# Turning the rows of the last gate product by DMA in two planes of 16-bit words

## The reference, cut to what matters

```
x = x + (silu(h @ w_ffn_gate) * (h @ w_ffn_up)) @ w_ffn_down
gate = sigmoid(rmsnorm(x, ple_norm_g) @ w_ple_gate)      # (1024 x 1024) @ (1024 x 1024)
x = x + gate * (p @ w_ple_proj)                          # (1024 x 256) @ (256 x 1024)
out = rmsnorm(x, final_norm_g)
```

## Time and profile before

| | us |
|---|---|
| median of 3 runs (1244.51 to 1245.03) | 1244.6 |
| the profiled execution | 1244.54 |
| its span in the trace | 1242.8 |
| PE busy | 1228.3 (99%) |
| DVE busy | 714.8 (58%) |
| POOL busy | 511.4 (41%) |
| ACT busy | 472.5 (38%) |

### The profile page before, as it was taken

The page is one execution under the profiler, slowest core; times in us unless marked ns, Lnnn a source line. Parts: engine busy times, 40 slices in busy tenths (PEclk is TensorE's granted clock), DMA queues, the critical chain, the costliest instruction groups (busy, mean ns, idle before and its releaser), DMA issues.

```text
span 1242.8 us, 16468 instructions
## 1 busy us (share of the span) xinstructions
PE 1228.3 (99%) x5998; PEld 1037.0 (83%) x5998; DVE 714.8 (58%) x1160; ACT 472.5 (38%) x866; POOL 511.4 (41%) x508
## 2 busy tenths in 40 slices
PE   9999999999999999999999999999999999999997
PEld 8888888788998888888888888888888888888886
DVE  5644444366664347745544455444499999954434
ACT  6622222245554125533333333333354344424422
POOL 2533443351000004455543455433499889810001
PEclk9999999999999999999999999999999999999999
DMA  9511101001031400333342342422554455420002
GB/s 334 176 34 42 45 1 43 1 1 34 18 105 50 152 1 1 85 119 115 98 127 77 94 127 85 128 94 80 182 199 161 167 169 188 151 85 1 1 34 102
DMA packets 102063, 115.14 MB, mean 93 GB/s; under 512 B 4832, under 2 KB 67936, under 8 KB 101984
## 3 DMA queue, kind: packets, MB, share of 16 engines
q1 hardware_dynamic: 101552, 113.57, 28.2%
q10 hardware_dynamic: 432, 0.54, 0.1%
HBM read 90.49 MB, written 23.59 MB: 92 GB/s over the span
## 4 chain that ended last, share of the span: by engine, by line
PE 93%; DMA 2%; ACT 2%; DVE 1%; issue 1%; SPq 1%; POOL 0%; POOLq 0%; ACTq 0%; DVEq 0%
PE PS L1729 11%; PE PS L1728 11%; PE PS L1727 11%; PE PS L206 7%; PE PS L208 7%; PE PS L207 7%; PE PS L2061 5%; PE PS L2062 5%; PE PS L2063 5%; PE PS L1046 3%; PE PS L1069 3%; PE PS L2438 2%; PE PS L2440 2%; PE PS L2439 2%; PE PS L2453 2%; PE PS L880 1%
## 5 line engine op out<-in xcount | busy, mean ns | idle before, releaser
L206 PE MATMUL PS<-WF,HTH 128*128 128x512 f32 (+1 forms) x448 | 176.6, 394 | 1.2 <-DVE WF L184 0.9
L208 PE MATMUL PS<-WF,HTL 128*128 128x512 f32 (+1 forms) x448 | 173.3, 387 | 0.0
L207 PE MATMUL PS<-WF,HTH 128*128 128x512 f32 (+1 forms) x448 | 172.9, 386 | 0.0
L1448 DVE TENSOR_TENSOR X<-X,PS 128x512 f32<-128x512 f32 x172 | 110.2, 679 | 54.4 <-PE PS L208 37.2
L1727 PE MATMUL PS<-HTH,WF 128*128 128x512 f32 x336 | 130.7, 389 | 0.0
L1728 PE MATMUL PS<-HTL,WF 128*128 128x512 f32 x336 | 130.7, 389 | 0.0
L1729 PE MATMUL PS<-HTH,WF 128*128 128x512 f32 x336 | 130.7, 389 | 0.0
L1660 DVE TENSOR_TENSOR WF<-RAW,WF 128x512 fp32r<-128x512 f32 x63 | 69.8, 1109 | 77.2 <-ACT WF L1650 77.2
L206 PEld LDWEIGHTS PS<-WF,HTH 128*128 128x128 f32 x448 | 84.2, 188 | 17.5 <-issue 1.2
L1727 PE MATMUL PS<-WF 128*128 128x512 f32 x252 | 98.0, 389 | 0.0
L1728 PE MATMUL PS<-WF 128*128 128x512 f32 x252 | 98.0, 389 | 0.0
(11 more groups left out here) (268 smaller groups left out, 2778.4 us busy)
## 6 DMA issues: line engine op xcount, KB each, us to landing
hid<-TMP SPq DMA_DIRECT2D x74, 256.0 KB, 2.3
TMP<-hid SPq DMA_DIRECT2D x25, 512.0 KB, 4.5
RAW<-in_w_ffn_gate SPq DMA_DIRECT2D x22, 512.0 KB, 4.1
RAW<-in_w_ffn_up SPq DMA_DIRECT2D x22, 512.0 KB, 5.3
RAW<-in_w_ffn_down SPq DMA_DIRECT2D x22, 512.0 KB, 4.3
X<-in_x SPq DMA_DIRECT2D x16, 512.0 KB, 6.0
RAW<-in_w_in SPq DMA_DIRECT2D x32, 256.0 KB, 3.9
TAB<-hid SPq DMA_DIRECT2D x9, 512.0 KB, 4.7
```

The costliest lines, as they stand in the source:

```text
L206: nc.tensor.matmul(dst, HTH[:, k, tok], w_h, start=(k == 0), stop=False)
L207: nc.tensor.matmul(dst, HTH[:, k, tok], w_l, start=False, stop=False)
L208: last = nc.tensor.matmul(dst, HTL[:, k, tok], w_h, start=False, stop=(k == K - 1))
L1448: nc.vector.tensor_tensor(x, x, src, ALU.add).then_inc(done, 1)
```

## The change

The transposes on TensorE are left out. In their place, for each token tile, in this order:

1. POOL copies the 1024 words of 32 bits of a row of x into two planes of 1024 words of 16 bits (`x_split`), in TMP.
2. SP issues one DMA transpose of the 128 x 2048 words of 16 bits (`sp_x_turn`), into 16 blocks of 128 x 128, also in TMP.
3. POOL copies the two planes back together into words of 32 bits (`x_join`), in GB.
4. ACT and DVE make high and low part from there, at the same places of their queues as before (`joined_hi`, `joined_lo`).

There is one buffer for each of the three steps. The squares of ACT write their unused result to PSUM instead of TMP, and the load of the final gain into GB moves behind the last low part. Two semaphores of the attention (`a_mask`, `a_rec`) are merged into others with doubled counts; the order there is the same.

```
+        x_halves, x_turned, x_joined = sem("x_halves"), sem("x_turned"), sem("x_joined")
...
         def sp_6(e):
...
-            e.wait_ge(e_lo, 6)
+            for t in range(T):
+                sp_x_turn(e, t)
+            e.wait_ge(n_ple.lo, 2 * T)
             e.dma_start(GB[:, :], t_in["final_norm_g"].partition_broadcast(P)).then_inc(s_gain, 16)
...
+        def words_of(x):
+            return x.bitcast(U16).rearrange("p (n b) -> p b n", b=2)
+        HALVES, HALVES_T, JOINED = tmp(2048, 1024).bitcast(U16), tmp(3072, 1024).bitcast(U16), GB[:, :]
+        def x_split(e, t):
             if t == 0:
                 e.wait_ge(r_alo, STEPS)
+            else:
+                e.wait_ge(x_turned, 16 * t)
+            e.wait_ge(f_added, N_DOWN + 2 * t + 2)
+            nc.gpsimd.tensor_copy(HALVES.rearrange("p (b n) -> p b n", b=2), words_of(X3[:, t, :])).then_inc(x_halves, 1)
...
+        def sp_x_turn(e, t):
+            e.wait_ge(x_halves, t + 1)
             if t:
+                e.wait_ge(x_joined, t)
+            e.dma_start_transpose(HALVES_T.rearrange("p (c n) -> p c n", n=P), HALVES).then_inc(x_turned, 16)
...
+        def x_join(e, t):
+            e.wait_ge(x_turned, 16 * t + 16)
+            if t:
+                e.wait_ge(n_ple.lo, 2 * t)
+            else:
+                e.wait_ge(e_lo, 6)
+            nc.gpsimd.tensor_copy(words_of(JOINED), HALVES_T.rearrange("p (b n) -> p b n", b=2)).then_inc(x_joined, 1)
...
+        def joined_hi(e, t):
+            e.wait_ge(x_joined, t + 1)
+            for j in range(2):
+                nc.scalar.copy(HTH[:, 4 * j:4 * j + 4, t * P:t * P + P], joined(j)).then_inc(n_ple.hi, 1)
+        def joined_lo(e, t):
...
         def pool_6(e):
+            x_split(e, 0)
             for t in range(T):
                 norm_rstd(e, n_ple, t, 48)
+                x_join(e, t)
+                if t < T - 1:
+                    x_split(e, t + 1)
...
-            def turn(t):
-                if t in (4, 6):
-                    ple_turn(e, t // 2 - 2)
-            pe_down(e, turn)
-            ple_turn(e, 2)
+            pe_down(e)
...
-                if u < 5:
-                    ple_turn(e, u + 3)
```

More of the change, by code:

```diff
@@ L16 @@
 I32 = mybir.dt.int32
+U16 = mybir.dt.uint16
 ALU = mybir.AluOpType
@@ L131, in __init__ @@
                     self.lo = sem(name + "_lo")
-        n_mix, n_ple = Norm("mix", rows=False, turned=False), Norm("ple", rows=False)
+        n_mix, n_ple = Norm("mix", rows=False, turned=False), Norm("ple", rows=False, turned=False)
         n_ffn, n_out = Norm("ffn", split=False), Norm("final", turned=False, split=False)
@@ L849, in build @@
         a_proj, a_hi, a_lo = sem("a_proj"), sem("a_hi"), sem("a_lo")
-        a_scores, a_mask, a_max, a_bias = sem("a_scores"), sem("a_mask"), sem("a_max"), sem("a_bias")
-        a_exp, a_rec, a_prob, a_turn = sem("a_exp"), sem("a_rec"), sem("a_prob"), sem("a_turn")
+        a_scores, a_max, a_bias = sem("a_scores"), sem("a_max"), sem("a_bias")
+        a_exp, a_prob, a_turn = sem("a_exp"), sem("a_prob"), sem("a_turn")
         a_pt, a_pv, a_o_hi, a_o_lo = sem("a_pt"), sem("a_pv"), sem("a_o_hi"), sem("a_o_lo")
@@ L1050, in pe_turn @@
             t = n % T
-            e.wait_ge(a_prob, n + 1)
+            e.wait_ge(a_prob, 2 * n + 2)
             e.wait_ge(a_pt, n)
@@ L1160, in dve_biggest @@
             nb, width = seen(t)
-            nc.vector.memset(src[0:CHUNK, nb - 1, width - CHUNK:width], MASKED).then_inc(a_mask, 1)
-            e.wait_ge(a_mask, n + 1)
+            nc.vector.memset(src[0:CHUNK, nb - 1, width - CHUNK:width], MASKED).then_inc(a_max, 1)
+            e.wait_ge(a_max, 2 * n + 1)
             nc.vector.tensor_reduce(ST[:, 74 + t % 2:75 + t % 2], src, mybir.AxisListType.XY if nb > 1 else AXX,
                                     ALU.max).then_inc(a_max, 1)
-            e.wait_ge(a_max, n + 1)
+            e.wait_ge(a_max, 2 * n + 2)
             nc.vector.tensor_scalar(ST[:, 76 + t % 2:77 + t % 2], ST[:, 74 + t % 2:75 + t % 2], -SCALE, None,
@@ L1179, in dve_divide @@
             e.wait_ge(a_exp, n + 1)
-            nc.vector.reciprocal(ST[:, 80 + t % 2:81 + t % 2], ST[:, 78 + t % 2:79 + t % 2]).then_inc(a_rec, 1)
-            e.wait_ge(a_rec, n + 1)
+            nc.vector.reciprocal(ST[:, 80 + t % 2:81 + t % 2], ST[:, 78 + t % 2:79 + t % 2]).then_inc(a_prob, 1)
+            e.wait_ge(a_prob, 2 * n + 1)
             p = tmp((t % 2) * 1024, (t + 1) * P)
@@ L2091, in down_lo, with pe_down @@
                                     ALU.subtract).then_inc(d_lo, 1)
-        def pe_down(e, more):
+        def pe_down(e):
             e.wait_ge(d_lo, STEPS + 4)
@@ L2109, in pe_down @@
                     last.then_inc(f_down, 1)
-                more(t)
         def pe_5(e):
@@ L2247, in sp_6, with joined @@
                 e.wait_ge(s_out[c], 16 * T // 4 + (16 if c == 3 else 0))
+        SINK = PS[:, 0:2, :].rearrange("p b n -> p (b n)")
         def ple_squares(e, t):
             e.wait_ge(f_added, N_DOWN + 2 * t + 2)
+            if t:
+                e.wait_ge(n_ple.squares, t)
+            norm_squares(e, n_ple, t, 48, X3[:, t, :], SINK)
+        def words_of(x):
+            return x.bitcast(U16).rearrange("p (n b) -> p b n", b=2)
+        HALVES, HALVES_T, JOINED = tmp(2048, 1024).bitcast(U16), tmp(3072, 1024).bitcast(U16), GB[:, :]
+        def x_split(e, t):
             if t == 0:
                 e.wait_ge(r_alo, STEPS)
-            if t:
[L2254 to L2259, removed]
+            else:
[4 more added lines that the diff above has]
+            e.wait_ge(x_halves, t + 1)
+            if t:
+                e.wait_ge(x_joined, t)
+            e.dma_start_transpose(HALVES_T.rearrange("p (c n) -> p c n", n=P), HALVES).then_inc(x_turned, 16)
+        def x_join(e, t):
+            e.wait_ge(x_turned, 16 * t + 16)
+            if t:
+                e.wait_ge(n_ple.lo, 2 * t)
+            else:
+                e.wait_ge(e_lo, 6)
+            nc.gpsimd.tensor_copy(words_of(JOINED), HALVES_T.rearrange("p (b n) -> p b n", b=2)).then_inc(x_joined, 1)
+        def joined(j):
+            return JOINED[:, j * HALF:(j + 1) * HALF].rearrange("p (k n) -> p k n", k=4)
+        def joined_hi(e, t):
[3 more added lines that the diff above has]
+        def joined_lo(e, t):
+            d = slice(t * P, t * P + P)
+            for j in range(2):
+                e.wait_ge(n_ple.hi, 2 * t + j + 1)
+                nc.vector.tensor_tensor(HTL[:, 4 * j:4 * j + 4, d], joined(j), HTH[:, 4 * j:4 * j + 4, d].bitcast(F32),
+                                        ALU.subtract).then_inc(n_ple.lo, 1)
         def p_part(t, y):
@@ L2285, in act_6 @@
                 if t in (5, 7):
-                    turned_hi(e, n_ple, (t - 5) // 2)
-            turned_hi(e, n_ple, 2)
+                    joined_hi(e, (t - 5) // 2)
+            joined_hi(e, 2)
             for t in range(T):
@@ L2290, in act_6 @@
                 if 1 <= t <= 5:
-                    turned_hi(e, n_ple, t + 2)
+                    joined_hi(e, t + 2)
                 if t >= 1:
@@ L2313, in act_6 @@
                 n = HALF // 2
-                nc.scalar.activation(tmp(2048, n), X3[:, T - 1, HALF + i * n:HALF + i * n + n], ACT.Square, scale=D ** -0.5,
+                nc.scalar.activation(SINK[:, 0:n], X3[:, T - 1, HALF + i * n:HALF + i * n + n], ACT.Square, scale=D ** -0.5,
                                      accum_out=LAST_SUM if i else ST[:, 112 + T - 1:112 + T]).then_inc(n_out.squares, 1)
@@ L2328, in squares_half @@
                 e.wait_ge(n_out.squares, half * T + t)
-            nc.scalar.activation(tmp(2048, HALF), X3[:, t, half * HALF:(half + 1) * HALF], ACT.Square, scale=D ** -0.5,
+            nc.scalar.activation(SINK[:, 0:HALF], X3[:, t, half * HALF:(half + 1) * HALF], ACT.Square, scale=D ** -0.5,
                                  accum_out=ST[:, 96 + 16 * half + t:97 + 16 * half + t]).then_inc(n_out.squares, 1)
@@ L2360, in dve_6 @@
                 if t in (5, 7):
-                    turned_lo(e, n_ple, (t - 5) // 2)
-            turned_lo(e, n_ple, 2)
+                    joined_lo(e, (t - 5) // 2)
+            joined_lo(e, 2)
             for t in range(T):
@@ L2365, in dve_6 @@
                 if 1 <= t <= 5:
-                    turned_lo(e, n_ple, t + 2)
+                    joined_lo(e, t + 2)
                 if t >= 1:
```

## The result

| | before | after |
|---|---|---|
| median, us | 1244.55 (1244.39 to 1245.03) | 1252.9 (1251.87 to 1253.29) |
| ratio to before | | 1.0065, 95% interval 1.005 to 1.008 |
| span of the profiled execution, us | 1242.8 | 1251.0 |

The change makes the kernel slower by 0.65%, some 8.3 us. The direction, the place and the mechanism were forecast; the forecast size was +30.8 us, more than three times too much.

What follows compares the result with a forecast made beforehand. TensorE was taken to bound the kernel. Saving 7.0 us of transposes against 37.8 us of waiting for the ring gave net +30.8 us, 1244.54 to 1275.3 us; range 1249 to 1360, slower 0.86.

Steps and rivals of the forecast that it cites:

- What bounds the kernel, and what is saved: TensorE, busy 99% of the span, bounds; removing 64 transposes, 8 tiles at 0.87 us, saves 7.0 us on the path.
- the ring: Per tile, POOL splits, SP's DMA transpose lands, POOL joins, without overlap between tiles; forecast period 11.8 us.
- S: POOL's split copy of a tile into planes, counted by elements: 2.5 us.
- D: DMA transpose of a tile, issue to landing: 7.0 us; chance 0.24 for above 12 us, 0.62 for 3 to 12.
- J: POOL's copy joining the two turned planes, counted by elements at the pace of its known copy: 2.1 us.
- Where the ring meets TensorE: Gate step 6 waits until eight rings have joined tile 7: starts at 1199.2 instead of 1168.4, 30.8 us late.
- the prediction's second formula: Short ring: tile 1's join waits for tile 0's low part; gate step 6 starts at 1123.4 + 6P.
- P: Period of the ring: S + D + J plus 0.2 us of handovers, 11.8 us, against 6.8 us per gate step.
- the branch of the long ring: Eight rings counted from the first split at 1102.1 decide: tile 7 joined at 1102.1 + 8 x 11.8 = 1196.5.
- The queue order: On ACT and DVE, tile t+2's parts stand ahead of step t-1's sigmoid and multiplication; costs one further ring, steps 2 to 6.
- the fast rival: The ring is short and hidden: up to the full 7.0 us gained, 1237.6; chance 0.09 for a gain above 2.5 us.
- The clock: TensorE's clock may fall in 5 us gaps per step, which absorb it; 0 to 5 us at the end, range only.

## Why the prediction was right in kind and wrong in size

- **What bounds the kernel, and what is saved: right.** With the ring out of the way 6.7 us are gained, where 8 x 0.87 = 7.0 were counted.
- **The ring and its serial order: right.** S, D and J follow each other in the chain, and overlapping them gives the gain.
- **The price of the transpose: the step that failed.** D was taken as 7.0 us and measured 4.2. The sum priced a packet at 55 ns, the mean over queue 1, whose packets average 1.1 KB, and took 128 for each DMA engine. The count was right (130), the price was not. The last transpose alone has 54.8% of 16 x 5.1 us for its 2080 packets, 21.5 ns each, and 130 x 21.5 ns = 2.8 us for an engine. They overlap a little: from the first start to the last pass 2.6 us, which leaves 1.6 of the 4.2 us outside the packets. A packet of a quarter of the bytes cost two fifths. Both estimates that the prediction drew from the Trainium skill (Advanced Engine Details and Errata, section X-Bar Transpose (TRN2), and VectorE: DVE Perf Modes, section The three transpose paths) are off here, to either side: 1.4 us for the transfer was 2.6, some 200 GB/s, and sixteen blocks are 4.2 us and not 20.9. The second took the page's time for one block sixteen times; here blocks after the first eight cost 0.15 us each.
- **The copies: right in sum.** By elements and not by bytes; 1.89 and 2.50 us where 2.5 and 2.1 were taken. The higher price sat on the wrong one: the split is not slowed in this ring, where it meets the low part of the tile before in part only (it is in the run with two buffers, 2.34 us), and the join writes with a step.
- **Where the ring meets TensorE: right for this size.** With D = 4.2 and the rest of its numbers the prediction's second formula gives P = 9.0, 1123.4 + 54 = 1177.4, +9.0 us; with the measured copies it is 1118.6 + 2.5 + 6 x 8.6 + 2.7 = 1175.4, +7.0; measured was 1176.33, one ring being 0.7 us longer. So with the price of the transpose put right, and nothing else, the forecast is +9.0 where +8.3 was measured. The size fell in a gap of the reasoning all the same: the forecast worked in the branch of the long ring, 8P from the first split, where 3.2 us too much in P count eight times, and its ends of +2 and +71 us showed how much hung on one unknown.
- **The queue order: right in kind.** It was named as one further ring, which would be 8.6 us; undoing it in full gave 6.2 of the 8.3 us back. What it can give is about the 6.8 us of a gate step and not a ring, since step 7 then waits for the tile that step 6 waited for. That the low part of p stands in the same order was not seen, nor that for a short ring the limit binds at step 2. By this the fast rival was priced too well: at P = 6.35 us it gave 3 us and not 7.
- **The clock: the reasoning held, the place was not foreseen.** The prediction had it fall in gaps of 5 us a step and be taken up by them. Gaps of 1.5 us a step left the granted clock full (1.00 from 1150 to 1170). It fell once, in a standstill of 7.45 us that was not forecast, and TensorE waited for the ring behind it all the same. In the run with two transposes, gaps of 2.9 to 3.8 us had it at 0.70 to 0.78, and they did take it up.

## What to carry to other kernels

When work is taken from the engine that is the bound and spread over a chain of other engines with one buffer each, the period of the chain is the sum of its links and not the longest; second buffers were worth more here (from +8.3 to -6.1 us, one for the join of tile 1 among them) than the cheaper copies (to -3) or half the transpose (to +2). Look then at what the consumers have queued behind the late result: the same order that costs at most 0.6 us with a short ring makes 6.2 of the 8.3 us lost with a ring of 8.6 us. And a long wait in a profile may only be the first place where a loss shows; if removing it makes an equal one appear later, the cause lies behind both.

## What was not expected of the hardware

A DMA transpose of 128 x 2048 words of 16 bits within SBUF lands in 4.2 us, of 128 x 1024 in 3.0; the first moves 0.52 MB as 2080 packets in 2.6 us, some 200 GB/s. A copy of 2048 words of 16 bits takes POOL 1.89 us reading with a step of two words, 2.50 writing with it, 2.13 writing in order out of two planes, and 1.04 us for the same bytes as words of 32 bits. DVE and POOL are slower beside each other. Of the two subtractions of 128 x 512 that make a low part from two SBUF operands, the one beside POOL's split took 1.66 us and the next 0.68 (DVE's timeline, windows 1130.4 to 1131.6 and 1132.2 to 1132.7):

```profile
1130.48 1.66 DVE L2296 TENSOR_TENSOR HTL<-GB,HTH 128x512 fp32r<-128x512 f32 x1 [6.31 <-ACT HTH L2290]
1132.07 0.68 DVE L2296 TENSOR_TENSOR HTL<-GB,HTH 128x512 fp32r<-128x512 f32 x1
```

The split was not slowed (1.89 us), but the small norm instructions of POOL behind it took 0.5 and 0.9 us instead of 0.2 and 0.55.
